# Moving two ACT copies of the state-space inputs ahead of one piece's softmax exponentials

## What is computed

```
proj = h @ even_w_in[e]
qa, ka, va, ub = jnp.split(proj, ...)
oa = chunk_band_attention(qa, ka, va, even_rel_bias[e])      # 8 heads of 64, softmax, relative bias
ob = s5_mixer(ub, ...)            # 32 groups of 16 channels, one 64-dim complex diagonal state per group
mix = jnp.concatenate([oa, ob], axis=-1) @ even_w_out[e]
```

## Time and profile before

| | |
|---|---|
| median of three runs | 1151.68 us |
| profiled execution | 1149.84 us |
| its span, first to last instruction | 1148.0 us |
| PE busy | 1128.0 us, 98% |
| DVE busy | 888.1 us, 77% |
| ACT busy | 551.3 us, 48% |
| POOL busy | 559.4 us, 49% |
| TensorE clock granted | 0.999 of full |
| tick 2 of the even attention, about | 98 to 107 us |

### The profile page before, as it was taken

One profiled execution on the slowest core, in us unless ns is written; L12 is line 12 of the kernel. 1 busy time (PEld: TensorE's weight loads), 2 busy tenths in 40 slices (PEclk: granted clock), 3 DMA queues, 4 the chain that ended last, 5 costly groups with the idle time before them and its releaser, 6 DMA issues.

```text
span 1148.0 us, 19245 instructions
## 1 busy us (share of the span) xinstructions
PE 1128.0 (98%) x7437; PEld 983.3 (86%) x7437; DVE 888.1 (77%) x1234; ACT 551.3 (48%) x864; POOL 559.4 (49%) x360
## 2 busy tenths in 40 slices
PE   7999999999999999999999999999999999999997
PEld 6877768899999999888887777777999999998886
DVE  8558653887888888995965787766987888889957
ACT  6335665245444554453455655533444544444540
POOL 6897614356577764013795222212576676760000
PEclk9999999999999999999999999999999999999999
DMA  8622326143333335226134221202523333352341
GB/s 214 185 79 87 109 72 202 37 129 111 96 106 113 92 111 180 96 92 220 47 120 127 57 71 40 75 1 74 147 80 105 111 111 100 104 163 96 98 122 74
DMA packets 161755, 122.04 MB, mean 106 GB/s; under 512 B 19409, under 2 KB 140281, under 8 KB 161665
## 3 DMA queue, kind: packets, MB, share of 16 engines
q1 hardware_dynamic: 161664, 120.82, 35.3%
HBM read 117.37 MB, written 3.43 MB: 105 GB/s over the span
## 4 chain that ended last, share of the span: by engine, by line
PE 93%; DVE 4%; POOL 1%; ACT 1%; issue 0%; DMA 0%; SPq 0%; DVEq 0%; ACTq 0%
PE ps L2320 18%; PE ps L2322 18%; PE ps L2321 18%; PE ps L2350 6%; PE ps L2352 6%; PE ps L2351 6%; PE ps L2343 4%; PE ps L2345 4%; PE ps L2344 4%; PE ps L2881 2%; PE ps L2892 2%; PE ps L2907 2%; POOL wlo L926 1%; PE ps L2357 1%; PE ps L2582 1%; PE ps L2925 1%
## 5 line engine op out<-in xcount | busy, mean ns | idle before, releaser
L926 POOL TENSOR_TENSOR wlo<-raw,whi 128x1024 fp32r<-128x1024 f32 x73 | 178.3, 2457 | 252.0 <-ACT whi L1081 243.8
L2320 PE MATMUL ps<-xhi,whi 128*128 128x256 f32 (+1 forms) x848 | 272.0, 321 | 0.7 <-DVE xlo L1573 0.6
L2322 PE MATMUL ps<-xhi,wlo 128*128 128x256 f32 (+1 forms) x848 | 266.8, 315 | 0.0
L2321 PE MATMUL ps<-xlo,whi 128*128 128x256 f32 (+1 forms) x848 | 266.7, 314 | 0.0
L2320 PEld LDWEIGHTS ps<-xhi,whi 128*128 128x128 f32 x848 | 161.6, 191 | 18.3 <-issue 6.4
L1005 POOL TENSOR_TENSOR wlo<-raw,whi 128x512 fp32r<-128x512 f32 x114 | 173.2, 1545 | 0.6 <-ACT whi L1371 0.4
L2320 PE MATMUL ps<-thi,whi 128*128 128x256 f32 x608 | 172.1, 283 | 0.0
L2321 PE MATMUL ps<-tlo,whi 128*128 128x256 f32 x608 | 172.1, 283 | 0.0
L2322 PE MATMUL ps<-thi,wlo 128*128 128x256 f32 x608 | 172.1, 283 | 0.0
L2322 PEld LDWEIGHTS ps<-xhi,wlo 128*128 128x128 f32 x848 | 161.7, 191 | 10.4
L2321 PEld LDWEIGHTS ps<-xlo,whi 128*128 128x128 f32 x848 | 161.8, 191 | 8.5
(11 more groups left out here) (324 smaller groups left out, 2482.1 us busy)
## 6 DMA issues: line engine op xcount, KB each, us to landing
raw<-in_ffn_w SPq DMA_DIRECT2D x126, 512.0 KB, 3.8
raw<-in_odd_w_in SPq DMA_DIRECT2D x22, 512.0 KB, 3.7
raw<-in_even_w_in SPq DMA_DIRECT2D x16, 512.0 KB, 4.6
t<-in_ffn_w SPq DMA_DIRECT2D x12, 512.0 KB, 6.7
h<-in_x SPq DMA_DIRECT2D x8, 512.0 KB, 5.4
raw<-in_even_w_out SPq DMA_DIRECT2D x8, 512.0 KB, 3.8
raw<-in_odd_w_out SPq DMA_DIRECT2D x8, 512.0 KB, 3.5
bias<-rel_scratch SPq DMA_DIRECT2D x8, 256.0 KB, 3.6
```

Source lines behind the costliest of these rows:

```text
L926: eng.tensor_tensor(lo, source_of(b), hi, ALU.subtract).then_inc(w_lo, 1)
L2320: eng.matmul(o_, w_hi_, x_hi_, start=start, stop=False)
L2321: eng.matmul(o_, w_hi_, x_lo_, start=False, stop=False)
L2322: return eng.matmul(o_, w_lo_, x_hi_, start=False, stop=stop)
```

## The change

In tick 2, and in that alone, ACT does the copies of (2, 0) and (2, 1) before `softmax_exp(3)` and not behind it. The other engines' streams are as before.

```
--- before.py
+++ after.py
@@ -559,6 +559,7 @@
         GLU_FIRST = {9: (0,), 10: (1,), 11: (2,)}
         Y_FIRST = 2
         QK_FIRST = (6,)
+        COPIES_FIRST = (2,)
 
         def aqk_runs(n):
             return [run for run in oqk_runs(n) if run[0] < 2 * AT]
@@ -1239,13 +1240,16 @@
 
             UPPER_AT = {-1: 13, 0: 14, 1: 15, 2: 16, 3: 17, 5: 18, 6: 19, 8: 20}
             for n in range(-1, A_PIECES):
+                if n in COPIES_FIRST:
+                    ssm_outs(SSM_BEFORE[n])
                 if n + 1 < A_PIECES and n not in QK_FIRST:
                     softmax_exp(n + 1)
                 for m in run_ends(aqk_runs(n)):
                     qk_out(m)
                 if n in QK_FIRST:
                     softmax_exp(n + 1)
-                ssm_outs(SSM_BEFORE.get(n, ()))
+                if n not in COPIES_FIRST:
+                    ssm_outs(SSM_BEFORE.get(n, ()))
                 if n >= 0:
                     turned_out(n)
                 ssm_outs(SSM_AT.get(n, ()))
```

## The result

The changed kernel takes 1155.24 us (median of 8 runs, 1153.85 to 1157.88), the kernel before 1151.60 (8 runs, 1151.22 to 1153.71): ratio 1.0035, 95% interval 1.0026 to 1.0044. It is slower by 3.6 us, 0.35%. The profiled execution took 1157.88 us (span 1156.1), the longest of the eight.

A forecast was written before the change was run, and what follows sets the result against it. PE, busy 98% of the span, was taken as the bound. It would win 1.36 us at the copies, but DVE and POOL alternating would make it late: net +2.0 to +3.6, taken at +2.8, giving 1154.5 us, range 1150.4 to 1155.5.

The forecast's parts named there:

- The copies: At L2483, ACT's winr and wini copies come before exp(3): PE wins 1.36 us, 0.35 of the stall stays.
- DVE and POOL change places: Near 114.5 us, earlier PE wakes POOL ahead of DVE's scalings; they alternate, and exp(5) starts at 125.8 against 120.23.
- The stall at a projection: At PE's next projection, a late qT copy loses about 0.7 of the 1.36 us if DVE is 1.2 late.
- The sum: All terms up to PE's lateness at L2472: +2.0 to +3.6 us, taken at +2.8.
- the full count: At L2472, DVE products all alternating with POOL, with no slips: PE starts at 128.9 instead of 125.50, +3.4 us.
- the forecast's case: From 114.5 us DVE and POOL alternate, PE waits at L2472 for yT: likeliest 1153.7 to 1155.3 us, chance 0.52.
- the forecast's own quarter: The part of the alternating case not above +2.3 us, counted as same; three quarters lay above.
- (b): DVE keeps POOL out from 114.47; toep at L2506 takes back the gain: 0 to +0.2 us, 1151.8, chance 0.22.
- (c): DVE slips through three or four times before POOL's wlo: PE +0.5 to +2 us, about 1152.9, chance 0.12.
- (a): PE keeps all or part of its 1.36 us from L2483, 0.65 if qT is late: 1150.3 to 1151.1, chance 0.14.

The follow-up runs named there:

- e3: Changed kernel plus 29 identity transposes on PE just ahead of the wni transposes of quarter 3; 1153.64 us, ratio 1.0016 to the kernel before.
- e7: The changed kernel measured and profiled once more, unaltered; 1156.27 us, ratio 1.0045 to the kernel before.
- e1: Changed kernel with ACT's exp(5) put behind the copy of (1, 6) in tick 4; 1153.74 us, ratio 1.0019 to the kernel before.
- e2: Changed kernel with POOL waiting, ahead of build_out(3, 0), for DVE's xsr and xsi of quarter 2; 1150.94 us, ratio 0.9993 to the kernel before.
- e4: Changed kernel with POOL's wait for DVE's xsr and xsi, and toep(2) sent ahead of the weight load; 1149.89 us, ratio 0.9988 to the kernel before.
- e5: The e4 kernel with ACT also copying qT ahead of exp(4) in tick 3; 1149.54 us, ratio 0.9988 to the kernel before.

## Why the prediction was right and wrong

**The copies: right.** L2487 was forecast at 104.33 and started at 104.36; exp(3) at 104.08, and it was 104.10. The wait fell to 0.38 (0.35 forecast).

**DVE and POOL change places: right.** POOL at 114.47 forecast, 114.50 measured; DVE's scalings from 114.6 to 114.7, measured 114.58. The scalings took 2.35 us (2.5 forecast), and from the first product to the end of xsi it was 126.68 + 0.95 - 120.84 = 6.8 (6.9 forecast). exp(5) came at 125.1 (125.8 forecast), the wni transposes at 128.18 (128.9 forecast): +2.68 for the forecast +3.4, and inside +2.0 to +3.6 even after the 0.2 at toep. The stall at a projection, 0.7 forecast, was 0.51.

**The size: wrong, by a term that was missing.** The sum ended with PE's lateness at the transposes. It forecast a new wait of 2 to 4 us on PE, took it as costing no more than its own length, and so put what follows at nothing: at half clock the next instructions cost 1.6 us more in one profile and 2.7 in another, and e3 shows that this hangs on PE being idle, since the transposes come as late there and the clock stays. With it the forecast +2.8 is +4.4 to +5.5, where +4.05 and +5.23 were measured as places and +3.64 and +5.15 as medians. In these ticks the trace of before had no row of it, as its longest idle there (1.71 us) left the clock at 1.0. It had one at its start, which the prediction did not look at:

```profile
6.17 3.42 PE L2357 MATMUL ps<-ident,h 128*128 128x128 f32 x16 [6.17 <-DMA h<-in_x]
```

Behind 6.17 us of idle, 16 transposes took 3.42 us, 0.21 each, with no gap between them, where four such have the next four 0.43 behind them, 0.11 each. Only the pace says so: the windows give no clock under 1.00 there. So the forecast should have stood open upwards. That the median, 1155.24, still lies under the range's top of 1155.5 is luck: the full count of the lateness at the transposes, 3.4, was 0.7 too high, which made room for part of the missing term, and the top itself is 0.2 above the sum (1151.68 + 3.6 = 1155.28). e7's median lies above it.

**The chances: wrong.** The most likely outcome by the chances was "within 0.2%", at 0.53, and slower had 0.40. With the missing term every loss of the forecast's case is beyond 2.3 us. That takes the forecast's own quarter out of the 0.53. The largest part of it, 0.34, came from rivals (b) and (c), that DVE might hold POOL off as at 115.83. In all four profiles in which POOL was not held back (the changed kernel twice, e1, e3) POOL started within 0.1 us ahead of the scalings and DVE alternated with it. So these rivals had too much. The Trainium skill's rule (SBUF — State Buffer, "Who interferes with whom": the pair is held for a whole instruction by whichever issued first) agrees with these four, in which one DVE product after the other ends 0.2 to 0.3 us behind a POOL instruction. With the row at 115.83, where POOL took 1.58 us instead of 0.63 and three of DVE's products (starts 115.84, 116.17 and 116.51) went ahead of it, it doesn't; no run was made for that, and it stays open.

**Rival (b)'s step was right though its case wasn't.** Its claim that toep, queued behind the load that waits for POOL, would be the next wait is what e2 shows, at 2.0 us; only with toep moved does PE keep its gain (e4). Rival (a)'s account, the gain less a stall for qT, is what e4 then gives, with a smaller stall: 1.36 less 0.51 (0.7 forecast), and the 0.17 that PE no longer waits for toep, are 1.02.

## What to carry to other kernels

Taking a stall off the bounding engine also moves forward whoever that engine wakes; look where the woken engine meets a third one, since the order of two engines can flip there and cost more than the stall gave (here POOL came 1.4 us behind DVE and then 0.1 us ahead of it, and PE lost 4.05 and 5.23 us for 1.33 won). An in-order queue turns such lateness into a stall where a small copy for the bounding engine stands behind a long chain's step; give copies that free a bank the first place. Price a new stall of several microseconds on TensorE with its clock, and after removing one, list in order what is late next (here ACT's order, then toep behind a weight load, then qT), as it paid in full only with the whole list: by the medians the edit alone cost 3.6 us, with its two companions it gains 1.3 (e4) and with the third 1.6 (e5).

## What the runs showed of the hardware that was not expected

TensorE's granted clock fell from 1.0 to 0.50 behind an idle time of 3.57 us, and behind one of 2.06 us in the head. It stayed at 1.0 behind 1.71 us (the kernel before) and behind 1.96 us (e2). Two profiles of one kernel, with the same idle time to 0.01 us, had PE at work at 0.50 for 3.41 and for 6.08 us, and lost 1.6 and 2.7 us by it.
